# A state-space layer's weight blocks in two stretches instead of four

## The reference

```
def ssd_mixer(h, conv_state, ssm_state, w_in, ...):
    z, xbc, dt = split(h @ w_in, [2048, 2048 + 3072])        # 1024 -> 5152 columns
    conv = conv_b + sum(ext[:, k:k + L] * conv_w[k] for k in range(4))
    xs, bs, cs = split(silu(conv), [2048, 2560])
    y, new_state = ssd_scan(xh, softplus(dt + dt_bias), -exp(a_log), bs, cs, ssm_state)
    y = y + xh * d_skip
    y = rmsnorm(y * silu(z))              # in 4 groups of 512 channels
    return y @ w_out, new_conv, new_state
```

## Time and profile before

| | us |
|---|---|
| median of 3 runs | 2440.27 |
| lowest and highest run | 2433.73, 2440.28 |
| the profiled execution, its time | 2427.95 |
| the profiled execution, its span | 2426.2 |
| mean granted clock of TensorE in it | 0.926 |
| PE busy in it | 2210.4 (91%) |
| PEld busy | 1968.6 (81%) |
| DVE busy | 1234.2 (51%) |
| ACT busy | 1017.1 (42%) |
| POOL busy | 436.1 (18%) |

### The profile page before, as it was taken

One profiled execution on the slowest core, in us unless ns is written; L12 is line 12 of the kernel. 1 busy time (PEld: TensorE's weight loads), 2 busy tenths in 40 slices (PEclk: granted clock), 3 DMA queues, 4 the chain that ended last, 5 costly groups with the idle time before them and its releaser, 6 DMA issues. The chain is left out here.

```text
span 2426.2 us, 38651 instructions
## 1 busy us (share of the span) xinstructions
PE 2210.4 (91%) x15123; PEld 1968.6 (81%) x15123; DVE 1234.2 (51%) x2108; ACT 1017.1 (42%) x1569; POOL 436.1 (18%) x428
## 2 busy tenths in 40 slices
PE   6899979999966898999977799789999999979999
PEld 4888869999965456999965466589998888879999
DVE  5666645554442234554436433255546566655554
ACT  3666654443341112443354111344434656644432
POOL 2211102441010002342000000024421111113330
PEclk9899989999985798999985599899999999989999
DMA  5244525555572442655564446156556244435654
GB/s 172 87 135 144 153 80 149 167 161 156 164 238 84 115 135 80 174 158 155 158 189 143 160 158 212 35 148 174 155 159 186 79 144 144 138 105 164 168 148 139
DMA packets 505226, 352.45 MB, mean 145 GB/s; under 512 B 13547, under 2 KB 486397, under 8 KB 504217
## 3 DMA queue, kind: packets, MB, share of 16 engines
q1 hardware_dynamic: 503906, 323.01, 45.7%
q0 software_dynamic: 1152, 27.13, 3.4%
HBM read 326.59 MB, written 50.63 MB: 155 GB/s over the span
## 5 line engine op out<-in xcount | busy, mean ns | idle before, releaser
L249 PE MATMUL ps<-xh,wh 128*128 128x288 f32 x2368 | 652.8, 303 | 16.3 <-ACT wh L213 16.2
L249 PE MATMUL ps<-xl,wh 128*128 128x288 f32 x2368 | 643.8, 298 | 0.0
L221 DVE TENSOR_TENSOR wl<-raw,wh 128x2048 fp32r<-128x2048 f32 (+3 forms) x241 | 501.3, 2082 | 242.0 <-ACT wh L213 242.0
L213 ACT ACTIVATE wh<-raw 128x2048 fp32r<-128x2048 f32 (+3 forms) x241 | 418.6, 1740 | 269.1 <-PE ps L257 229.7
L249 PEld LDWEIGHTS ps<-xh,wh 128*128 128x128 f32 x2368 | 452.7, 191 | 18.3 <-issue 14.2
L249 PEld LDWEIGHTS ps<-xl,wh 128*128 128x128 f32 x2368 | 452.3, 191 | 0.5
L257 PE MATMUL ps<-xh,wl 128*128 128x288 f32 x2368 | 353.3, 300 | 0.0
L257 PEld LDWEIGHTS ps<-xh,wl 128*128 128x128 f32 x2368 | 326.9, 190 | 2.3
L472 POOL TENSOR_TENSOR gh<-sg,ut 128x288 f32<-128x288 f32 x88 | 216.7, 2463 | 351.5 <-ACT sg L411 351.5
L249 PE MATMUL ps<-hh,wh 128*128 128x288 f32 x704 | 191.0, 296 | 0.0
L249 PE MATMUL ps<-hl,wh 128*128 128x288 f32 x704 | 190.9, 297 | 0.0
(11 more groups left out here) (318 smaller groups left out, 3112.6 us busy)
## 6 DMA issues: line engine op xcount, KB each, us to landing
raw<-in_ffn_w_in SPq DMA_DIRECT2D x176, 512.0 KB, 5.1
raw<-in_ssm_w_in SPq DMA_DIRECT2D x80, 512.0 KB, 4.8
raw<-in_ffn_w_out SPq DMA_DIRECT2D x64, 384.0 KB, 4.2
raw<-in_ffn_w_out SPq DMA_DIRECT2D x64, 320.0 KB, 3.4
H<-in_state_ssm SPq DMA_DIRECT2D x32, 512.0 KB, 7.4
out_ssm_sample<-H SPq DMA_DIRECT2D x32, 512.0 KB, 6.3
raw<-in_ssm_w_out SPq DMA_DIRECT2D x32, 512.0 KB, 5.3
Kp<-in_cache_diff_k SPq DMA_DIRECT2D x64, 256.0 KB, 4.1
```

Source lines behind the costliest of these rows:

```text
L213: act.activation(wts["hi"][:, s, 0:width], raw[:, s, 0:width], ACT.Copy).then_inc(hi_ready.sem, 1)
L221: dve.tensor_tensor(wts["lo"][:, s, 0:width], raw[:, s, 0:width], wts["hi"][:, s, 0:width].bitcast(F32), ALU.subtract).then_inc(lo_ready.s ...
L249: pe.matmul(out, W[0][:, kk, j, :], x_[:, k, :], stop=False, start=(part == 0 and kk == 0 and x_ is seg.hi), skip_group_check=True)
```

## The change

`stretch` takes eight k-tiles at a time instead of four:

```diff
         def stretch(kk):
 
-            return range(kk, min(kk + 4, lin.kk)) if kk % 4 == 0 else ()
+            return range(kk, min(kk + 8, lin.kk)) if kk % 8 == 0 else ()
```

## The result

| | before | changed | ratio, 95% interval |
|---|---|---|---|
| median of four runs each, us | 2440.28 | 2481.84 | 1.0167 [1.0123, 1.0211] |
| lowest to highest | 2433.73 to 2445.64 | 2471.11 to 2492.16 | |
| profiled execution | 2427.95 | 2478.55 | |

The account below looks back on a forecast made before the run. PE, without pause in the loop, bounds the kernel. Terms -3.8 + 9.3 + 12 + 3.9 = +21.4 us on the profiled 2427.95 give 2449.4; counted as +19.4 on the runs' mean 2438.1, 2457 us, range 2440 to 2477.

Parts of the forecast that it names:

- The view of the loop: Chunk loop: PE has no pause, so only stretch borders, answers losing their cover and TensorE's granted clock can act.
- Borders: Second stretch of either pair goes, saving its entry cost in 28 iterations: -3.8 us, between nothing and 7.6 gained.
- No wait in the ordinary iteration: Ordinary loop iterations: DVE and ACT answer before PE reaches either outer_half or the second spread; cost zero.
- Root: At k = 7 and 11, spread waits uncovered for ACT's logarithm: 4 x 2.33 = 9.3 us over both layers.
- The clock at root: Clock falls to 1.2 GHz about when the new root waits end: about 3.0 us each, 12 us for four.
- Chunk 0: Clock stays low behind spread(1) in layer 3 as in layer 0, so products take 5.67 us in both: +3.9 us.
- rival 3: Small work between hi and lo stretches, 5.3 us 28 times, lowers the clock by itself: some 2540 us; chance 0.04.
- my own sign: Forecast is wrong if k = 7 and 11 match their neighbours, or ordinary iterations change by over 0.3 us.
- The rival's price: Rival 3's cost: 3 us in each of 28 runs of small work, +84 us.
- No other stage should change: Expected sign in the profile: stages other than those the forecast names stay as they were.

Follow-up runs that it names:

- before_wide: The kernel before with only y_state's four columns streamed sixteen times over per matmul; 2428.98 us, ratio 0.9957 to before.
- wide_y: The changed kernel with each y_state matmul streaming its four columns sixteen times over (64 columns); 2450.10 us, ratio 1.0053 to before.
- hi_one: Against the kernel before, hi matmuls merged into one stretch of 32, lo matmuls left in two of eight; 2498.38 us, ratio 1.0259.

## Why the prediction was right or wrong

- **The view of the loop was right.** PE had no slack, the same work was moved, and only borders, lost cover and the clock could act.
- **Borders** (-3.8): right in kind, -0.11 us per iteration instead of -0.14, so -3.1.
- **No wait in the ordinary iteration**: right. `outer_half` and the second spread stand where forecast, PE has no pause.
- **Root** (9.3): right, 8.8. The chain from `sums_of_chunk` through ACT was as long as in the old trace.
- **The clock at root** (12): right in mechanism, all four fell; 10.1.
- **Chunk 0** (3.9): right in the products of both layers, 2.6 in all.
- **What failed** is the rejection of rival 3, "Runs of small work pull the clock down by themselves", with a chance of 0.04: the sum puts the clock in the ordinary iterations at nothing. I set against it that "from 331.6 to 345.1 only such work ran, with pauses, at 1.00 throughout". The row is right, but it doesn't carry that. The stretch is the mixer's last chunk, and `sums_of_chunk` and the same `y_state` open it. The first row below is that `y_state` in the kernel before. The two windows are the same chunk, in the same order, in the changed kernel, where the clock fell in it in both layers (here layer 0):

```profile
332.59 1.85 PE L1091 MATMUL ps<-BC,HT 128*128 128x4 f32 x16
```
```profile
355.90:359.10 3.20, 2.94 (x25) 2.42 (x23) 1.03 (x4) 0.45 (x2) 0.00 (x0) 1.00 0.00 0
359.30:365.90 6.60, 6.56 (x23) 4.62 (x24) 4.28 (x12) 0.60 (x2) 0.00 (x0) 0.50 0.34 99
```

- So the clock falls in some of such runs of small work and not in others (11 of the 24 in the loop), and I took one that stayed clear for proof that none falls. By my own sign ("if the ordinary ones change by more than 0.3 us") the forecast was wrong: they took 1.5 or 3.0 us more. The fall at 321.3 in the earlier trace rows also comes behind a `y_state`, but it says nothing on this: with wide `y_state` and the same pause before_wide has the clock fall there too, at 321.9.
- **The rival's price** was wrong as well: the clock fell in 11 of 24 ordinary iterations and not in 28, and cost 1.5 or 3 us each, 22 us and not 84. With this term beside the others the sum would have been 2480. The rival as worded was too wide, too: it is runs of small work with `y_state` in them (wide_y).
- **"No other stage should change"** failed with it: the last chunks took 7.3 us more.
- The Trainium skill's advice to do all k-tiles before the next wait, so that TensorE stays warm ("TensorE: Matmul & The Clock Gate", "HAM oscillation"), came out the other way here, at 1.0167. The longer stretch is fine by itself (wide_y, 1.0053 with the waits for root still there), but it leaves a longer run without one.

## What to carry to other kernels

When weight matmuls are gathered, look at what is then left between them: the small work loses its cover for waits, and the clock sees a longer run of little work. A row that says PE is busy does not say that the clock takes it for work; matmuls of a few columns with a full weight load each are the suspects. What falls in 11 of 24 cases can stay away in the one stretch of the old trace that one looks at: before a rival is struck out by a quiet stretch, ask how many of its kind there are.

## What the runs showed of the hardware

- Sixteen matmuls of 4 columns with 128x128 weights leave PE busy for 1.8 us and still let the clock go from 2.4 to 1.2 GHz beside other small work, in 11 of 24 iterations; with 64 columns they take 0.05 us more and none of the 24 had a fall. The same edit made the kernel before 0.4% faster, 0.9957 [0.9931, 0.9982].
- One program's executions differ by over 1% through the clock alone: 19 runs of before from 2424.49 us at a mean clock of 0.929 to 2452.55 at 0.917.
- Small work does not bring a low clock back soon: 10.2 us of it ran at 0.50 in the kernel before (321.3 to 331.5). Where a lo stretch of sixteen weight matmuls followed, the late ordinary falls lasted 3.4 us each (the changed kernel, 7 of 7); with eight in its place they lasted 6.8 or 10.2 in 14 of 15 (hi_one).
